# The up-projections of an MLA branch as three-term float32r products, with GpSimd making the low parts

## The reference

```python
proj = rms_norm(h, attn_norm) @ w_in            # 1024 -> 4640, split into seven parts
q  = (rms_norm(q_lat, g) @ w_uq)                # latents of 768 -> 8 heads x 96
kv = (rms_norm(kv_lat, g) @ w_ukv)              # latents of 256 -> 8 heads x (64 + 64)
o_a = causal attention over 8 heads, q and k normed per head, last 32 of 96 rotated (k's shared)
o_b = differential attention: 8 sub-heads of 64, normed and rotated, pairs subtracted, normed
h = h + (sigmoid(gate_a) * (o_a @ w_a) + sigmoid(gate_b) * (o_b @ w_b)) @ w_out
h = h + moe(rms_norm(h, g))                     # 32 experts, top 4, each 1024 -> 2048 -> 1024
```

## Time and profile before

| | us |
|---|---|
| median of 3 runs | 1157.66 (1156.36 to 1158.23) |
| the profiled execution itself | 1157.1 |
| its span, first to last instruction | 1155.2 |

### The profile page before, as it was taken

How to read it: one execution, slowest core, us unless ns; L and a number is a source line. 1 busy time by engine, 2 the same in 40 slices (tenths; PEclk the granted TensorE clock), 3 DMA queues, 4 the chain that set the end, 5 groups by cost and what they waited for, 6 DMA issues and landing times.

```text
span 1155.2 us, 12817 instructions
## 1 busy us (share of the span) xinstructions
PE 1107.6 (96%) x5124; PEld 513.3 (44%) x5124; DVE 303.5 (26%) x552; ACT 206.9 (18%) x355; POOL 36.1 (3%) x44
## 2 busy tenths in 40 slices
PE   8999999999999999999999898989898999999997
PEld 8867788744343434343434242424242424242422
DVE  4566766521211111121211111111111202020212
ACT  6646565411010101010100000000000101010100
POOL 1005310000000000000000000000000000000000
PEclk9999999989999999999999999999999999999999
DMA  9654237799999999999999999999999999999997
GB/s 368 268 182 145 74 110 295 299 414 371 406 427 421 427 428 428 428 431 427 428 428 428 431 427 428 428 428 431 427 428 428 428 431 427 428 428 429 428 427 289
DMA packets 34542, 439.10 MB, mean 380 GB/s; under 512 B 3984, under 2 KB 4112, under 8 KB 6704
## 3 DMA queue, kind: packets, MB, share of 16 engines
q1 hardware_dynamic: 33840, 433.55, 90.0%
q10 hardware_dynamic: 672, 5.12, 1.1%
HBM read 437.60 MB, written 1.05 MB: 380 GB/s over the span
## 4 chain that ended last, share of the span: by engine, by line
PE 73%; DMA 24%; ACT 2%; DVE 1%; issue 1%; SPq 0%; ACTq 0%; DVEq 0%
DMA ring<-in_expert_w 24%; PE bank L742 20%; PE bank L765 20%; PE bank L424 12%; PE bank L717 5%; PE bank L690 5%; PE bank L643 4%; PE bank L407 3%; PE bank L474 1%; PE bank L510 1%; PE bank L485 1%; DMA tok_r<-in_x_turned 0%; PE bank L715 0%; PE bank L535 0%; ACT gate_r L976 0%
## 5 line engine op out<-in xcount | busy, mean ns | idle before, releaser
L742 PE MATMUL bank<-ring,feat_r 128*64 128x512 f32 x1504 | 334.5, 596 | 9.7 <-DMA ring<-in_expert_w 9.7
L742 PEld LDWEIGHTS bank<-ring,feat_r 128*64 128x64 f32 x1504 | 103.2, 137 | 231.6 <-issue 206.8
L765 PE MATMUL bank<-ring,late_r 128*64 128x512 f32 x768 | 173.3, 596 | 12.4 <-DMA ring<-in_expert_w 12.0
L424 PE MATMUL bank<-ring_s,feat_s 128*128 128x512 f32 (+2 forms) x448 | 136.8, 388 | 2.5 <-DVE ring_s L1138 2.3
L1392 DVE TENSOR_SCALAR gate_r<-bank 128x512 f32<-128x512 f32 x32 | 22.1, 692 | 433.2 <-PE bank L742 433.2
L742 PE MATMUL bank<-pool_r,feat_r 128*64 128x512 f32 x512 | 114.6, 595 | 9.5 <-DMA pool_r<-in_expert_w 9.5
L1414 DVE TENSOR_TENSOR acc_r<-bank,acc_r 128x512 f32<-128x512 f32 x64 | 44.3, 692 | 259.7 <-PE bank L717 259.7
L1082 ACT ACTIVATE gate_r<-gate_r 128x512 f32<-128x512 f32 x32 | 20.2, 630 | 482.3 <-DVE gate_r L1392 482.3
L765 PEld LDWEIGHTS bank<-ring,late_r 128*64 128x64 f32 x768 | 54.0, 137 | 117.5 <-issue 114.9
L424 PEld LDWEIGHTS bank<-ring_s,feat_s 128*128 128x128 f32 x448 | 81.5, 191 | 17.5 <-issue 5.0
L424 PE MATMUL bank<-ring_s 128*128 128x512 f32 (+2 forms) x224 | 84.9, 379 | 0.0
(11 more groups left out here) (187 smaller groups left out, 598.5 us busy)
## 6 DMA issues: line engine op xcount, KB each, us to landing
ring<-in_expert_w SPq DMA_DIRECT2D x140, 2048.0 KB, 31.3
pool_r<-in_expert_w SPq DMA_DIRECT2D x48, 2048.0 KB, 33.0
ring<-in_head_w SPq DMA_DIRECT2D x23, 1024.0 KB, 5.0
ring<-in_head_w SPq DMA_DIRECT2D x7, 768.0 KB, 9.2
ring<-in_expert_w SPq DMA_DIRECT2D x4, 1024.0 KB, 33.5
gate_r<-in_expert_w ACTq DMA_DIRECT2D x1, 2048.0 KB, 9.0
late_r<-in_expert_w ACTq DMA_DIRECT2D x1, 2048.0 KB, 14.7
ring<-in_head_w SPq DMA_DIRECT2D x2, 576.0 KB, 15.0
```

Of the source, the lines that this page charges most:

```text
L424: mm = pe.matmul(banks[m][:, 0:cols], featT[left][:, first + k, m * P:(m + 1) * P], right[:, k - k0, :], start=(k == 0 and left == 0 and r ...
L742: mm = pe.matmul(b[e * SLOTS:(e + 1) * SLOTS, :], xT[:, k, e * SLOTS:(e + 1) * SLOTS], w[:, e, g, :], start=False, stop=(k == KD - 1), ski ...
L765: mm = pe.matmul(bank[4 + h][e * SLOTS:(e + 1) * SLOTS, :], aT[k // 4][:, k % 4, e * SLOTS:(e + 1) * SLOTS], w[:, q, e, :], start=(k == 0) ...
```

## The change

`w_uq` and `w_ukv` become split products too. Their high parts are cast by ScalarE, their low parts are subtracted by GpSimd, and the turned latents get a low part from VectorE. High parts of all chunks now take the three buffers in strict chunk order, by chunk number and not by split number. VectorE's splits of chunks 14 and 15 and ScalarE's casts for them move behind this work. The low part of the latents lies in the upper half of `gate_r`, as `gate_s`.

```diff
+UP = [n for n, c in enumerate(HEAD) if c[0] in ("w_uq", "w_ukv")]
...
-        latT = v3(latT_r, KQ + KKV)
+        latT = v3(pool_s[:], KQ + KKV), v3(gate_s[:, NM * D:], KQ + KKV)
...
-        def split_views(i):
-            n = SPLIT[i]
+        def split_views(n):
             _, _, nk, _, cols = HEAD[n]
-            hi = (HEAD_RING + i % BUFFERS) * SLOT
+            hi = (HEAD_RING + n % BUFFERS) * SLOT
             lo = (n % HEAD_RING) * SLOT
             return ring_s[:, hi:hi + nk * cols], ring_s[:, lo:lo + nk * cols]
...  GpSimd, before its norm_rotate
+            for n in UP:
+                _, _, nk, _, cols = HEAD[n]
+                hi, lo = split_views(n)
+                pool.wait_ge(sem("hi_ready"), n + 1)
+                pool.tensor_tensor(lo, head_slot(n, nk * cols), hi, ALU.subtract).then_inc(sem("up_ready"), 1)
...  TensorE
+            pe.wait_ge(sem("latT_ready"), 4)
             HQ = HA * QK_A // 2
-            for i in range(KQ // 2):
-                arrive(n0 + i)
-                w = head_view(n0 + i)
+            def up_part(b, n, k, first, m, c, at, ends):
+                hi, lo = (v3(v, HEAD[n][2]) for v in split_views(n))
+                for left, right in ((0, hi), (0, lo), (1, hi)):
+                    mm = pe.matmul(b, latT[left][:, k, m * P:(m + 1) * P], right[:, at, c],
+                                   start=(first and left == 0 and right is hi), stop=(ends and left == 1),
+                                   skip_group_check=True)
+                return mm
+            for i, n in enumerate(UP[:-1]):
+                pe.wait_ge(sem("up_ready"), i + 1)
                 for h, b in enumerate(bq):
                     for m in range(NM):
                         for k in (2 * i, 2 * i + 1):
-                            mm = pe.matmul(b[m][:, 0:HQ], latT[:, k, m * P:(m + 1) * P], w[:, k - 2 * i, h * HQ:(h + 1) * HQ],
-                                           start=(k == 0), stop=(k == KQ - 1), skip_group_check=True)
+                            mm = up_part(b[m][:, 0:HQ], n, k, k == 0, m, slice(h * HQ, (h + 1) * HQ), k - 2 * i, k == KQ - 1)
                 mm.then_inc(ring_used, 1)
...  the same for w_ukv, behind up_ready >= len(UP)
...  ScalarE
-            def split_hi(i, halves=1):
-                n = SPLIT[i]
+            def chunk_hi(n, halves=1):
                 act.wait_ge(head_landed[n % HEAD_RING], 16 * (n // HEAD_RING + 1))
-                if i >= BUFFERS:
-                    act.wait_ge(ring_used, SPLIT[i - BUFFERS] + 1)
+                if n >= BUFFERS:
+                    act.wait_ge(ring_used, n - BUFFERS + 1)
...
             for m in range(NM):
                 act.wait_ge(sem("lat_turned"), m + 1)
                 ...copies to latT[0]
-            split_hi(10)
-            split_hi(11)
+            chunk_hi(UP[0])
+            chunk_hi(UP[1])
             ...copies of DK
+            chunk_hi(UP[2])
             ...squares of q and k
-            split_hi(12)
             ...square roots
+            chunk_hi(UP[3])
             ...copies of the product of w_uq
+            split_hi(10)
+            split_hi(11)
             ...copies of the product of w_ukv
+            split_hi(12)
             ...copies of the transposed q and k
...  VectorE
-            for i in range(9, 12):
-                split_lo(i)
+            split_lo(9)
+            for m in range(NM):
+                for i in range(2):
+                    dve.wait_ge(sem("unit_copied"), 9 + 2 * m + i)
+                    c = slice(m * P, (m + 1) * P)
+                    tt(latT[1][:, 4 * i:4 * i + 4, c], v3(bank[2 * m + i][:], 4), latT[0][:, 4 * i:4 * i + 4, c],
+                       ALU.subtract).then_inc(sem("latT_ready"), 1)
             ...sums of squares, norm_rotate twice
-            split_lo(12)
+            for i in range(10, 13):
+                split_lo(i)
```

More of the change, by code:

```diff
@@ L126, in build @@
         with nc.sbuf_tensor("ring_s", [P, RING * SLOT], F32R) as ring_s, \
-             nc.sbuf_tensor("feat_s", [P, KD * SEQ], F32R) as feat_s:
+             nc.sbuf_tensor("feat_s", [P, KD * SEQ], F32R) as feat_s, \
+             nc.sbuf_tensor("acc_0", [P, NM * D], F32), nc.sbuf_tensor("tok_0", [P, NM * D], F32), \
+             nc.sbuf_tensor("gate_s", [P, NM * 2 * D], F32R) as gate_s, \
+             nc.sbuf_tensor("pool_s", [P, SLOT], F32R) as pool_s:
             pass
@@ L224, in slot @@
             return ring[:, (s - EXTRA) * DOUBLE:(s - EXTRA + 1) * DOUBLE] if s < WIDE else once[s - WIDE]
-        def head_view(n):
+        def split_views(n):
             _, _, nk, _, cols = HEAD[n]
-            return v3(head_slot(n, nk * cols), nk)
-        def split_views(i):
-            n = SPLIT[i]
-            _, _, nk, _, cols = HEAD[n]
-            hi = (HEAD_RING + i % BUFFERS) * SLOT
+            hi = (HEAD_RING + n % BUFFERS) * SLOT
             lo = (n % HEAD_RING) * SLOT
@@ L407, in turn @@
                 return pe.transpose(dst, src, ident[0:rows, 0:rows])
-            def arrive(n):
-                pe.wait_ge(head_landed[n % HEAD_RING], 16 * (n // HEAD_RING + 1))
             def split_part(banks, n, ks, ms=range(NM)):
@@ L419, in split_part @@
                 pe.wait_ge(sem("lo_ready"), 2 * i + (2 if ks[-1] >= k0 + nk // 2 else 1))
-                hi, lo = (v3(v, nk) for v in split_views(i))
+                hi, lo = (v3(v, nk) for v in split_views(n))
                 for m in ms:
@@ L465, in _ @@
             pe.wait_ge(sem("unit_copied"), 2 * 6)
-            n0 = chunk_index("w_uq", 0, 0)
+            pe.wait_ge(sem("latT_ready"), 4)
             HQ = HA * QK_A // 2
-            for i in range(KQ // 2):
-                arrive(n0 + i)
-                w = head_view(n0 + i)
+            def up_part(b, n, k, first, m, c, at, ends):
[7 more added lines that the diff above has]
+                pe.wait_ge(sem("up_ready"), i + 1)
                 for h, b in enumerate(bq):
@@ L473, in _ @@
                         for k in (2 * i, 2 * i + 1):
-                            mm = pe.matmul(b[m][:, 0:HQ], latT[:, k, m * P:(m + 1) * P], w[:, k - 2 * i, h * HQ:(h + 1) * HQ],
-                                           start=(k == 0), stop=(k == KQ - 1), skip_group_check=True)
+                            mm = up_part(b[m][:, 0:HQ], n, k, k == 0, m, slice(h * HQ, (h + 1) * HQ), k - 2 * i, k == KQ - 1)
                 mm.then_inc(ring_used, 1)
-            n0 = chunk_index("w_ukv", 0, 0)
-            arrive(n0)
-            w = head_view(n0)
+            pe.wait_ge(sem("up_ready"), len(UP))
             for h in range(2):
@@ L484, in _ @@
                     for k in range(KKV):
-                        mm = pe.matmul(b[m][:], latT[:, KQ + k, m * P:(m + 1) * P], w[:, k, h * HALF:(h + 1) * HALF],
-                                       start=(k == 0), stop=(k == KKV - 1), skip_group_check=True)
+                        mm = up_part(b[m][:], UP[-1], KQ + k, k == 0, m, slice(h * HALF, (h + 1) * HALF), k, k == KKV - 1)
             mm.then_inc(ring_used, 1)
@@ L840, in split_hi @@
                     c = slice(a * nk * cols // halves, (a + 1) * nk * cols // halves)
-                    ins = act.copy(split_views(i)[0][:, c], head_slot(n, nk * cols)[:, c])
+                    ins = act.copy(split_views(n)[0][:, c], head_slot(n, nk * cols)[:, c])
                     if a == halves - 1:
@@ L845, in split_hi @@
                         ins.then_inc(sem("first_hi"), 1)
+            def split_hi(i, halves=1):
+                chunk_hi(SPLIT[i], halves)
             act.wait_ge(sem("gain_landed"), 16)
@@ L895, in _ @@
                 for i in range(2):
-                    act.copy(latT[:, 4 * i:4 * i + 4, m * P:(m + 1) * P], v3(bank[2 * ((4 + m) % 4) + i][:], 4))\
+                    act.copy(latT[0][:, 4 * i:4 * i + 4, m * P:(m + 1) * P], v3(bank[2 * ((4 + m) % 4) + i][:], 4))\
                        .then_inc(sem("unit_copied"), 1)
-            split_hi(10)
-            split_hi(11)
+            chunk_hi(UP[0])
+            chunk_hi(UP[1])
             act.wait_ge(ring_used, chunk_index("w_in", 4, O_DK) + 1)
@@ L1130, in split_lo @@
                 _, _, nk, _, cols = HEAD[n]
-                hi, lo = split_views(i)
+                hi, lo = split_views(n)
                 if i == 0 and halves == (0,):
@@ L1134, in split_lo @@
                 else:
-                    dve.wait_ge(sem("hi_ready"), i + 1)
+                    dve.wait_ge(sem("hi_ready"), n + 1)
                 for a in halves:
```

## The result

The changed kernel takes 1164.28 us (median of 5 runs, 1160.51 to 1164.9) against 1157.16 before (5 runs): a ratio of 1.0045, interval 1.0028 to 1.0062, so 3.2 to 7.2 us slower; the two medians lie 7.1 apart, at the upper end of that. Six more runs of it later had a median of 1162.56 against 1157.59, ratio 1.0043 (1.0028 to 1.0059). The profiled execution took 1164.28, with a span of 1162.1.

The account below looks back on a forecast made before the run. The weight stream paces the expert stage; the head's length moves its start and the end. Later v start +1.95 and clock +2.0 give +4.0 on 1157.1, 1161.1; median 0.56 higher, written 1161.5; range 1156.5 to 1164.6, own 1159.4 to 1163.3.

Parts of the forecast that it names:

- TensorE's products: w_uq and w_ukv in the head: 18.0 us as reduced-precision products instead of 22.35, 4.4 less if all is ready.
- GpSimd's price: GpSimd's four low-part subtractions in the head: 3.1 us for 1536 columns, 4.1 for 2048.
- VectorE held: VectorE's norm-and-rotate passes: GpSimd's fourth subtraction excludes VectorE for a whole instruction, which loses 4.1 us.
- Late start of the passes: VectorE's reciprocal ahead of its norm-and-rotate passes moves from 63.95 to 64.85, +0.9, behind ScalarE's third cast.
- End of the passes: VectorE's two norm-and-rotate passes end at 82.3 instead of 77.27.
- Start of v: TensorE's v product in the differential branch starts at 84.6 instead of 82.67, +1.95 us.
- The clock: TensorE's granted clock falls to half speed in the v product after its thin stretch: 2.0 us lost, ends 0 and 3.4.
- (c): Rival: GpSimd needs 7.2 us for 2048 columns, v starts at 87.7; time 1164.6, chance 0.09.
- (a): Rival: no clock fall at v, or one that hits no work; only +1.95, time 1159.6, chance 0.16.
- (b): Rival: GpSimd doesn't hold VectorE in the passes, v starts at 80.5, -2.1; time 1155.5, chance 0.14.
- (d): Rival: the end doesn't follow the head, since the weight stream bounds the rest; time 1157.7, chance 0.05.

Follow-up runs that it names:

- experiment 8: Changed kernel with the four high parts in idle tiles and all low parts subtracted by VectorE, none by GpSimd: 1152.48 against 1157.59 us, ratio 0.9958.
- Experiment 1: Changed kernel with w_ukv's high part cast early to a free tile and its low part subtracted by VectorE: 1156.15 against 1157.78 us, ratio 0.9988.
- experiments 2 to 4: Kernel before plus one GpSimd instruction in VectorE's passes: in order, two-input subtraction, write only, one-input scaling; single runs 1158.3, 1157.42 and 1156.81 us.
- experiment 11: The changed kernel again, unaltered, for more runs: 1162.56 against 1157.59 us; a table behind it compares kernels at the same mean clock.
- experiment 10: Kernel before with 42 unused identity transposes on TensorE, 4.6 us of work, making the rest of the head later: 1164.19 against 1157.59 us, ratio 1.0059.
- experiment 7: Changed kernel with the four high parts in idle tiles, GpSimd still subtracting, VectorE's other splits back in place: 1160.47 against 1157.78 us, ratio 1.0019.

## Why the prediction was right

**TensorE's products**: 12.7 for w_uq (58.5 to 71.2; 12.5 forecast), the w_ukv product then started at 71.55 and ended at 77.1. 18.0 forecast for both, 17.99 in experiment 8.

**GpSimd's price**: 3.1 and 4.1 forecast from the line through two rows, 3.50 and 4.61 measured. The figure from the Trainium skill (GPSIMD Engine Reference, 3.1 Elementwise), 4497 ns for 2048 fp32 columns, was nearer than my line.

**VectorE held**: 4.1 forecast, 5.72 - 1.29 = 4.4 measured, in one instruction, as the earlier trace rows had it. Experiment 1 takes GpSimd's instruction out and the 4.4 are gone; experiments 2 to 4 put one in and VectorE is held again if it reads. The Trainium skill (SBUF — State Buffer, Who interferes with whom) states that a VectorE instruction with two SBUF inputs contends with a GpSimd instruction that reads SBUF, and not with one that only writes it. All three synthetic cases agree (4.18 and 3.31, against 0). The prediction took from there that the second is blocked fully. With two inputs on either side it was; with one input on GpSimd's side VectorE got on 1.2 before GpSimd had ended, and there the measurement decides.

**Late start of the passes**: 64.85 forecast, 64.78 measured. **End of the passes**: 82.3 and 82.5. **Start of v**: 84.6 and 84.94. So the step that decided came out within 0.4.

**The clock** is the term that was mis-sized. I put 2.0 on its fall at v. In the profile half speed lasted 3.4 us there and took 1.65 from TensorE: 0.8 in v (6.26 for 5.49) and 0.9 in the 8 transposes ahead of it (1.91 for 1.03). The 0.9 cost nothing, because TensorE would have spent it waiting for the split of the v chunk. In the second profile v lost 2.05 (7.54). What I left out is that the granted clock differs between executions at other places too: from the end of the head to the first expert product the traces took either 16.6 or 18.2, and the expert stage (from the first expert product to the end of the span) took 917.7 to 918.2 with the fall near 356 and 915.2 to 917.0 without, in the mean 2.0 less. The profiled execution had the dear variant of both, and differs from the one of before by 1.65 and 2.2 there. Without them its 6.9 would be 3.0, and my +4.0 lies between. By the estimate behind experiment 11, 2.7 in all go with the lower clock.

**The number.** 1157.1 + 4.0 + 0.56 is 1161.7 and not the 1161.5 that I wrote, a slip of 0.2. The forecast's own range, 1159.4 to 1163.3, holds the second median (1162.56) and not the first (1164.28). The first lies in the stated range only because that reached to 1164.6, for rival (c), which didn't come. The mechanism was right, but that the first number is inside is luck.

**Rivals**: (a) no fall: out, 0.73 in the row. (b) VectorE not held: out by experiments 1 and 2. The 104.31 row that spoke for it was one where GpSimd waited: its instruction beside it, recorded from 104.29, lasted 2.93, 1.1 more than the 1.83 that one of 768 columns took with no two-input VectorE instruction beside it (at 119.81 in the kernel after). (c) 7.2 for the last subtraction: out, 4.61. (d) the end doesn't follow: out by experiment 10 and by the table behind experiment 11.

## What to carry to other kernels

Before giving GpSimd elementwise work beside VectorE, add up the time in which either of them reads SBUF in a way that meets the other: with two inputs on both sides they take turns by whole instructions, so the sum, not the larger, has to fit, and the same subtraction is half as long on VectorE (1.75 against 3.50). An engine that is idle in the profile isn't free if its work stops one that is 3.65 us from the critical path. When a product gets cheaper, look at what was hidden behind it: here TensorE's 4.4 were saved from the first version on, and experiment 8 got them for the whole kernel (4.0 at the same clock) with idle tiles for the high parts and all subtractions on VectorE. The tiles alone didn't do it (experiment 7).

When two medians differ by a few us in a thousand, compare the mean granted clock of the executions too before explaining the difference by the edit.

## What the runs showed that I had not expected

- Cutting GpSimd's instruction into eight makes the turns finer but the total longer (8.71 for 4.61), so it moves the wait to whoever needs GpSimd's result.
- A GpSimd instruction with one SBUF input of 2048 columns took 5.65 in VectorE's passes, longer than one with two (4.81), and held VectorE for 3.31 of them.
- The granted clock fell to half speed in the expert stage with TensorE without an idle moment, in a run of small products, half of them with 32 rows; in other executions of the same work it stayed at 1.00.
